# Another order of the 24 products within each panel of the gates and the up projection, 26 orders in one kernel

## What is computed

```python
xn = _rmsnorm(h, norm1_g[l])
proj = xn @ w_in[l]                      # 2048 x (branches, then 3 x 2048 columns of gates)
...                                      # FoX attention, short convolution, GLA: three branches
ya = oa @ w_a_o[l]; yb = ob @ w_b_o[l]; yc = oc @ w_c_o[l]      # each 1024 -> 2048
mix = sigmoid(g_a + b_a) * ya + sigmoid(g_b + b_b) * yb + sigmoid(g_c + b_c) * yc
h = h + mix @ w_o[l]                     # 2048 -> 2048
u = _causal_dwconv(_rmsnorm(h, norm2_g[l]) @ w_up[l], mlp_conv_w[l])    # 2048 -> 2 x 5632
u_gate, u_up = jnp.split(u, 2, axis=-1)
h = h + (jax.nn.silu(u_gate) * u_up) @ w_down[l]                # 5632 -> 2048
```

## Time and profile before

| | |
|---|---|
| median of 3 runs | 1747.1 us (1746.53 to 1747.22) |
| profiled execution, span from the first to the last instruction | 1745.1 us |
| what the median has over that span | 2.0 us |
| PE busy | 1734.3 us, 99% of the span |
| PEld busy | 1680.7 us, 96% |
| DVE, ACT, POOL busy | 64%, 44%, 15% |
| mean share of time in which the DMA engines were busy | about 60% |
| granted clock of PE | 0.999 of full speed |

### The profile page before, as it was taken

One profiled execution on the slowest core, in us unless ns is written; L12 is line 12 of the kernel. 1 busy time (PEld: TensorE's weight loads), 2 busy tenths in 40 slices (PEclk: granted clock), 3 DMA queues, 4 the chain that ended last, 5 costly groups with the idle time before them and its releaser, 6 DMA issues.

```text
span 1745.1 us, 34098 instructions
## 1 busy us (share of the span) xinstructions
PE 1734.3 (99%) x13429; PEld 1680.7 (96%) x13429; DVE 1117.8 (64%) x1607; ACT 763.7 (44%) x921; POOL 263.3 (15%) x494
## 2 busy tenths in 40 slices
PE   9999999999999999999999999999999999999998
PEld 8999999999999999999999999999999999888886
DVE  6857766667565554555556687777777777554454
ACT  6635444354354444444444444334444444343433
POOL 3153332630530000000000043321000000000000
PEclk9999999999999999999999999999999999999999
DMA  8567557666565655556645566666555565665654
GB/s 232 169 180 186 168 149 198 176 175 178 153 184 181 189 178 178 175 182 194 201 159 192 181 195 192 204 200 192 183 182 181 180 186 180 223 190 189 189 192 134
DMA packets 310296, 320.62 MB, mean 184 GB/s; under 512 B 17353, under 2 KB 285133, under 8 KB 310093
## 3 DMA queue, kind: packets, MB, share of 16 engines
q1 hardware_dynamic: 296861, 311.01, 58.2%
q0 software_dynamic: 12928, 7.80, 2.0%
q10 hardware_dynamic: 432, 0.79, 0.1%
HBM read 311.10 MB, written 2.11 MB: 179 GB/s over the span
## 4 chain that ended last, share of the span: by engine, by line
PE 99%; DVE 0%; DMA 0%; ACT 0%; SPq 0%; issue 0%; ACTq 0%; DVEq 0%
PE ps L1435 27%; PE ps L1437 27%; PE ps L1436 27%; PE ps L1693 5%; PE ps L1692 5%; PE ps L1691 5%; PE ps L1526 0%; DMA xb<-in_x_dram 0%; PE ps L1540 0%; PE ps L1565 0%; PE ps L1555 0%; PE ps L1556 0%; PE ps L1584 0%; PE ps L1585 0%; DVE xl L941 0%; DVE lo L896 0%
## 5 line engine op out<-in xcount | busy, mean ns | idle before, releaser
L896 DVE TENSOR_TENSOR lo<-raw,hi 128x1024 fp32r<-128x1024 f32 x584 | 709.9, 1229 | 494.4 <-ACT hi L627 490.2
L1435 PE MATMUL ps<-xh,hi 128*128 128x260 f32 (+1 forms) x3328 | 945.8, 284 | 0.2 <-DVE xl L941 0.2
L1437 PE MATMUL ps<-xh,lo 128*128 128x260 f32 (+1 forms) x3328 | 941.7, 283 | 0.0
L1436 PE MATMUL ps<-xl,hi 128*128 128x260 f32 (+1 forms) x3328 | 936.5, 281 | 0.0
L627 ACT CAST hi<-raw 128x1024 fp32r<-128x1024 f32 x584 | 604.8, 1048 | 671.8 <-PE ps L1437 539.0
L1436 PEld LDWEIGHTS ps<-xl,hi 128*128 128x128 f32 x3328 | 626.6, 188 | 0.2
L1435 PEld LDWEIGHTS ps<-xh,hi 128*128 128x128 f32 x3328 | 625.2, 188 | 1.3 <-issue 0.4
L1437 PEld LDWEIGHTS ps<-xh,lo 128*128 128x128 f32 x3328 | 624.7, 188 | 0.0
L610 POOL DMA_DIRECT2D hT<-h2b x128 | 69.6, 553 | 604.3 <-DVE h2b L1289 599.7
L1693 PE MATMUL ps<-lo,act_h 128*128 128x512 f32 x350 | 138.5, 396 | 0.0
L1692 PE MATMUL ps<-hi,act_l 128*128 128x512 f32 x350 | 137.3, 392 | 0.0
(11 more groups left out here) (298 smaller groups left out, 1383.6 us busy)
## 6 DMA issues: line engine op xcount, KB each, us to landing
raw<-in_w_in_dram SPq DMA_DIRECT2D x224, 512.0 KB, 3.6
raw<-in_w_up_dram SPq DMA_DIRECT2D x176, 512.0 KB, 4.6
raw<-in_w_down_dram SPq DMA_DIRECT2D x88, 512.0 KB, 4.7
raw<-in_w_o_dram SPq DMA_DIRECT2D x32, 512.0 KB, 3.4
raw<-in_w_in_dram SPq DMA_DIRECT2D x32, 256.0 KB, 4.2
raw<-in_w_a_o_dram SPq DMA_DIRECT2D x16, 512.0 KB, 4.3
raw<-in_w_b_o_dram SPq DMA_DIRECT2D x16, 512.0 KB, 3.3
raw<-in_w_c_o_dram SPq DMA_DIRECT2D x16, 512.0 KB, 3.3
```

Of the source, the lines that this page charges most:

```text
L896: nc.vector.tensor_tensor(part(ph, i, q, lo_all), raw[:, s, :], part(ph, i, q, hi_all).bitcast(F32), ALU.subtract).then_inc(lo_ready, 1)
L1435: nc.tensor.matmul(acc, w_hi, mh, start=first and j == 0, stop=False)
L1436: nc.tensor.matmul(acc, w_hi, ml, start=False, stop=False)
L1437: ins = nc.tensor.matmul(acc, w_lo, mh, start=False, stop=last and j == KJ - 1)
```

## The change

`use_panel` stays as it is for BR and WO. GT and UP call a new function, `use_ordered`, which takes the 24 products of a panel from a list of (half, row, kind). Each of the 18 panels of a GT trip and each of the 8 panels of an UP trip has its own list, the same in every trip. Each list holds the same 24 products once. The lists are of six families:

- `by_row`: as before, half, row, kind, with the rows in another order
- `by_kind`: half, kind, row: four products of one kind, one for each row, then the next kind
- `in_turns`: half, pair of rows, kind, row of the pair
- `swing`: as `by_row`, with the second half's rows backwards
- `by_six`: row, half, kind
- `by_two`: high and rest-of-weights products of half 0 row by row, then the rest-of-activations products of both halves in turn, then those of half 1

The first product of a half in the panel's list carries `start`, the last one `stop`; the last product of all signals `panel_used`, and the wait for `lo` stands ahead of the first, as before. What any product reads and where it adds up is unchanged.

```diff
@@ -1420,6 +1420,47 @@
+            KINDS = ((hi, 0), (hi, 1), (lo, 0))
+            HIGH, LOW_X, LOW_W = range(3)
+
+            def by_row(*rows):
+                return [(m, j, kind) for m in range(2) for j in rows for kind in range(3)]
+
+            def by_kind(*rows):
+                return [(m, j, kind) for m in range(2) for kind in range(3) for j in rows]
+
+            def by_two(*rows):
+                passes = (((0, HIGH), (0, LOW_W)), ((0, LOW_X), (1, LOW_X)), ((1, HIGH), (1, LOW_W)))
+                return [(m, j, kind) for both in passes for j in rows for m, kind in both]
+
+            def by_six(*rows):
+                return [(m, j, kind) for j in rows for m in range(2) for kind in range(3)]
+
+            def swing(*rows):
+                return [(m, j, kind) for m in range(2) for j in (rows[::-1] if m else rows) for kind in range(3)]
+
+            def in_turns(*pairs):
+                return [(m, j, kind) for m in range(2) for pair in pairs for kind in range(3) for j in pair]
+
+            UP_ORDERS = (by_row(0, 1, 3, 2), by_row(0, 2, 1, 3), by_row(0, 2, 3, 1), by_row(0, 3, 1, 2),
+                         by_row(3, 2, 1, 0), swing(0, 1, 2, 3), by_six(0, 1, 2, 3), by_two(0, 1, 2, 3))
+            GT_ORDERS = (by_kind(0, 1, 2, 3), by_kind(0, 1, 3, 2), by_kind(0, 2, 1, 3), by_kind(0, 2, 3, 1),
+                         by_kind(0, 3, 1, 2), by_kind(0, 3, 2, 1), in_turns((0, 2), (1, 3)), in_turns((0, 1), (2, 3)),
+                         in_turns((0, 3), (1, 2)), by_two(0, 3, 2, 1), by_two(0, 2, 1, 3), by_six(0, 3, 2, 1))
+            BO_ORDERS = (by_two(0, 1, 3, 2), by_two(0, 2, 3, 1), by_two(0, 3, 1, 2), swing(0, 2, 1, 3), swing(0, 1, 3, 2),
+                         by_six(0, 2, 1, 3))
+
+            def use_ordered(ph, i, q, st, moving, n, first, last, order):
+
+                pe.wait_ge(lo_ready, ph.panel(i, q) + 1)
+                s = ph.slot(q)
+                for at, (m, j, kind) in enumerate(order):
+                    weights, side = KINDS[kind]
+                    own = [k for k in range(len(order)) if order[k][0] == m]
+                    ins = nc.tensor.matmul(pset(st, n)[:, m, :], tiles(weights, s, j, m), moving(j)[side],
+                                           start=first and at == own[0], stop=last and at == own[-1])
+                ins.then_inc(panel_used, 1)
+
...
-                    use_panel(GT, i, q, st, mv, NC, kq == 0, kq == last)
+                    use_ordered(GT, i, q, st, mv, NC, kq == 0, kq == last, (GT_ORDERS + BO_ORDERS)[q])
...
-                    use_panel(UP, i, q, st, x_window(kq * KJ, C0, NC), NC, kq == 0, kq == 3)
+                    use_ordered(UP, i, q, st, x_window(kq * KJ, C0, NC), NC, kq == 0, kq == 3, UP_ORDERS[q])
```

## The result

The changed kernel takes 1751.66 us (median of 8 runs, 1750.83 to 1752.21), the kernel before 1747.15 us on the same chips. The ratio is 1.0028, with a 95% interval of 1.0018 to 1.0037: slower by 4.5 us, a little more than the 0.2% that can be told from no change.

What follows compares the result with a forecast made beforehand. PE was taken as never waiting in GT or UP, so the distance between product starts sets the time. Terms summed to +1.3 us on a 1745.1 us span, plus 2.0 us to the median: 1748.4 us, range 1740 to 1756 us.

Steps and rivals of the forecast that it cites:

- What bounds the kernel: GT and UP: PE never waits there; time is the number of products times 118.8 ns between starts.
- The row j changes more often: GT and UP panels: more row changes between products cost 0 to 1.2 us; taken as 0.
- Halves in turn: `by_six` and `by_two` panels: about 660 more PSUM bank changes, taken as 0; 6.6 us if each cost 10 ns.
- kinds apart: `by_kind` and `by_two`: separating products with the same `hi` tile loses nothing, as each had its own weight load; 0.
- Rows in other orders: GT and UP: new row steps could cost or gain 9 us (1%), but 26 lists average out; taken as 0.
- Each panel starts in another list's state: 320 GT and UP panels: entry from another list costs -3.2 to +5.8 us; taken as +4 ns a panel, +1.3 us.
- A: Whole kernel: no more than the sum, within 3.5 us of before, 1748.4 us; chance 0.37.
- rival B: GT and UP slower, since steady rows 0, 1, 2, 3 were a good case: 5.8 to 9 us, 1753 to 1756; chance 0.32.
- The signs: Stretches within 15 and 10 products, UP and GT ends within 3 us; wrong if prices exceed 1% or lie one-sided.
- C: GT and UP faster, since the order before was poor: 3 to 6 us gained, 1742 to 1744 us; chance 0.24.
- The plain float32 products: Two products, 258 and 256 columns: 428 ns at two periods a column against 0.43 us, so next to nothing added.
- The fixed gap over the columns: Panel products: 2.5 ns over the columns gives 110.8 ns at 260 columns against 118.8 measured; no order has a price.

Runs made afterwards that it cites:

- moving_fixed: Changed kernel with its 26 lists, but every GT and UP product reads row 0 as moving tile; all panels take 2880 ns.
- stationary_shift: Changed kernel's 26 lists, moving tile always row 0, stationary tile of row j starting 64 j bytes earlier; panels take 2847 to 2892 ns.
- k0312_everywhere: Kernel before, with by_kind(0, 3, 1, 2) in all panels of BR, GT, WO and UP; 1748.98 us against 1746.75 (1.0013).

## Why the prediction was right, and where its steps were not

- *What bounds the kernel.* Right: no wait of PE appeared in GT or UP, and 4.9 of the span's 5.2 us are longer distances between starts there.
- *The row j changes more often: 0.* Right. `by_kind`, with a new row at each product, is among the cheapest families (11 ns on average), `by_row`, with the old number of changes, costs 16 ns; and `by_kind(0, 1, 2, 3)` by itself is 13 ns a panel quicker than the order before, with three times its changes. The rows that it was read from were poor ones, though: they give a product's duration, not the distance to the next start. From the starts, that distance is 119.0 ns behind products of line 1437, 120.1 behind 1435 and 117.6 behind 1436.
- *Halves in turn: 0; kinds apart: 0.* Right, and shown by `moving_fixed`, where `by_two` and `by_six` take 2880 ns as the others do.
- *Rows in other orders: 0, by averaging.* This is the term that was mis-sized, and with the hand-over it makes the whole result. 26 lists did not average to the order before; the mean is +15 ns a panel, 0.5%, 24 of the 26 above, one level, one below. The bound of 1% from the earlier trace rows held for the mean (it would be 29 ns), not for single lists (+50, +38 and +32 ns).
- *Each panel starts in another list's state: +4 ns.* That a panel's time hangs on what stands before it was right, the size too small for some: `by_kind(0, 1, 2, 3)` costs +11 ns behind the list that it follows in the changed kernel and -13 ns behind itself. The two terms can't be parted for all lists, since only four lists were seen following themselves for long at their true addresses.
- *Which rival.* I took A, 1748.4 us, as the likeliest, and rival B came true, the mildest case of it: slower by 4.5 us, near the 5.8 us that the disturbed panel of the earlier trace rows gave it. That is in part luck: one panel behind 272-column ones says nothing of a list's own price, and the lists' run from -18 to +50 ns. The sum gave 1.3 us of the 4.5. The range of 1740 to 1756 us held the time by its width, A's own range up to 1751 did not.
- *The signs.* It called itself wrong if lists had prices beyond 1% or all lay on one side: three do, and 24 of 26 do. The two stretches hold 16 and 17 products fewer, where 10 and 15 were allowed, and UP ends 5.1 us later, not within 3. Panels that differ from list to list, the same in every trip, came true. By its own signs the working failed at the averaging, though the time lies in the range.
- *B's reason.* "The steady repetition of rows 0, 1, 2, 3 was a good case" is half right: 2853 ns is below the mean of the lists, but the same rows taken kind by kind give 2840 ns, so C's reason, that the order before was a poor one, was half right too. That reading in ascending addresses is what keeps it short was not shown; 0, 3, 1, 2 is as quick.
- *The plain float32 products.* The earlier trace rows are two matmuls of 258 columns, not of 258 and 256; at two periods a column that is 430 ns for the 0.43 us, and the conclusion stays.
- *The fixed gap over the columns.* The formula of the Trainium skill ("TensorE: Matmul & The Clock Gate", Back-to-back issue gap) for an isolated warm matmul gives an estimate of 110.8 ns at 260 columns, and no order has it. At 240 columns it gives 102.5 ns; the run with narrower tiles shows 111.6. The same section of the Trainium skill says that in a stream of weight loads and matmuls both set the spacing; `stationary_shift`, where the loads' addresses alone move a panel from 2880 ns to 2847 to 2892, agrees.

The same page of the Trainium skill (Part 2, step 1) says that loading the next tile's weights doesn't steal SBUF read bandwidth from the running matmul. No run here measures that bandwidth, but the load is not without effect on the matmuls: in `stationary_shift`, with moving tiles that never change, the stationary tiles' start alone moves a panel between 2847 and 2892 ns. Whether the two reads meet in SBUF or behind it, in the array, no run here tells.

## What to carry to other kernels

When an engine is never idle and each of its instructions still takes longer than its work, read the distance from start to start over one period of the loop: it may hang on where operands lie and in which order, and then an order is worth a try. Measure such an order in the stretch in which it will run, and let it run there alone: a list's price behind other lists says little, and one list can have two steady times, by how it was entered. A survey of many variants in one kernel gives their spread in one trace, but its total is no forecast for any of them.

## What the runs showed of the hardware

- Panels of F32R products of 260 columns repeat to 1 ns in the kernel before, over 126 panels of GT's loop and 168 of UP's, while ACT and DVE work and the DMA engines are busy 60% of the time. The steady distances seen at the kernel's own addresses were 118.3, 118.9, 120.0 and 120.8 ns a product (panels of 2840, 2853, 2880 and 2900 ns).
- One order can settle at 118.3 or at 120.0 ns, and stay there (`k0312_everywhere`: 158 panels of GT's loop and WO at 120.0, the last 174 of UP at 118.3).
- The distance depends on where both tiles start. Over 16 moving starts, 16 bytes apart, panels take 2842 to 2907 ns, and 256 bytes on the distance comes back (seen at two of the starts); with the stationary starts alone moved, 2847 to 2892 ns.
- Between 252 and 244 columns the distance falls from 117.8 to 112.2 ns, 5.6 ns for 8 columns (3.3 ns at 2.4 GHz), and is 111.6 ns from 240 to 192 columns. A narrower tile gains nothing by that: a column costs 0.460 ns at 244 columns and 0.58 at 192, against 0.455 to 0.465 at 260, by the order.
- Not settled: why the two starts matter, and whether the weight load and the moving tile meet in a part of the chip that they share. That would need the two read separately. A row pitch that is a multiple of 256 bytes was not tried on true data.
